# Filler products ahead of the FFN: 11 float32 products of ones replaced by 60 float32r products of real operands

## What is computed

```
    mixed = (jax.nn.sigmoid(g_hg) * y_hg + jax.nn.sigmoid(g_da) * y_da) @ w_out[l]
    x = x + rms_norm(mixed, norm_mix_post[l])

    h = rms_norm(x, norm_ffn_pre[l])
    gate, up = jnp.split(h @ w_ffn_up[l], 2, axis=-1)
    ffn = (jax.nn.silu(gate) * up) @ w_ffn_down[l]
    x = x + rms_norm(ffn, norm_ffn_post[l])
```

## Time and profile before

| | us |
|---|---|
| median of 3 timed runs | 2039.4 (2038.42 to 2040.06) |
| span of the profiled execution | 2038.8 |
| TensorE products busy | 2028.0 (99% of the span) |
| VectorE busy | 1043.2 (51%) |
| ScalarE busy | 820.0 (40%) |
| mean granted TensorE clock | 0.999 of full |

### The profile page before, as it was taken

The page is one execution under the profiler, slowest core; times in us unless marked ns, Lnnn a source line. Parts: engine busy times, 40 slices in busy tenths (PEclk is TensorE's granted clock), DMA queues, the critical chain, the costliest instruction groups (busy, mean ns, idle before and its releaser), DMA issues.

```text
span 2038.8 us, 38346 instructions
## 1 busy us (share of the span) xinstructions
PE 2028.0 (99%) x14816; PEld 1915.0 (94%) x14816; DVE 1043.2 (51%) x1331; ACT 820.0 (40%) x1091; POOL 74.5 (4%) x119
## 2 busy tenths in 40 slices
PE   9999999999999999999999999999999999999999
PEld 9999888888888888899999999999999999999998
DVE  7443555646546465665546744434444445445445
ACT  6233443434434354354345433333333333445444
POOL 1001010000100000000000000000000000000000
PEclk9999999999999999999999999999999999999999
DMA  8867888988889888876544444444444444444441
GB/s 296 167 231 236 306 330 317 355 302 338 331 315 352 306 334 330 319 275 237 171 143 140 151 145 152 132 158 154 153 145 143 145 161 148 145 154 143 155 146 52
DMA packets 123982, 444.13 MB, mean 218 GB/s; under 512 B 14581, under 2 KB 18709, under 8 KB 123856
## 3 DMA queue, kind: packets, MB, share of 16 engines
q1 hardware_dynamic: 112720, 402.31, 55.4%
q0 software_dynamic: 9968, 39.48, 6.6%
q10 hardware_dynamic: 1232, 1.47, 0.2%
HBM read 423.28 MB, written 22.54 MB: 219 GB/s over the span
## 4 chain that ended last, share of the span: by engine, by line
PE 98%; DVE 1%; DMA 1%; ACT 0%; SPq 0%; issue 0%; DVEq 0%
PE ps L407 24%; PE ps L408 24%; PE ps L409 24%; PE ps L1769 5%; PE ps L1770 5%; PE ps L1768 5%; PE ps L881 3%; PE ps L915 3%; PE ps L890 1%; DMA raw<-w_hg 0%; PE ps L707 0%; PE ps L694 0%; DVE ffn L1730 0%; PE ps L667 0%; PE ps L644 0%; PE ps L673 0%
## 5 line engine op out<-in xcount | busy, mean ns | idle before, releaser
L366 DVE TENSOR_TENSOR w_lo<-raw,w_hi 128x1024 fp32r<-128x1024 f32 x416 | 505.4, 1224 | 543.9 <-ACT w_hi L361 289.4
L407 PE MATMUL ps<-x_hi,w_hi 128*128 128x320 f32 x1536 | 485.2, 316 | 1.6 <-DVE w_lo L366 1.6
L408 PE MATMUL ps<-x_hi,w_lo 128*128 128x320 f32 x1536 | 475.3, 309 | 0.0
L409 PE MATMUL ps<-x_lo,w_hi 128*128 128x320 f32 x1408 | 435.0, 309 | 0.0
L407 PE MATMUL ps<-h_hi,w_hi 128*128 128x320 f32 x1400 | 433.1, 309 | 0.0
L408 PE MATMUL ps<-h_hi,w_lo 128*128 128x320 f32 x1400 | 433.0, 309 | 0.0
L409 PE MATMUL ps<-h_lo,w_hi 128*128 128x320 f32 x1400 | 433.0, 309 | 0.0
L361 ACT ACTIVATE w_hi<-raw 128x1024 fp32r<-128x1024 f32 x236 | 247.2, 1059 | 424.5 <-PE ps L409 415.8
L407 PEld LDWEIGHTS ps<-x_hi,w_hi 128*128 128x128 f32 x1536 | 289.1, 188 | 38.6 <-issue 31.6
L408 PEld LDWEIGHTS ps<-x_hi,w_lo 128*128 128x128 f32 x1536 | 289.4, 188 | 0.1
L409 PEld LDWEIGHTS ps<-x_lo,w_hi 128*128 128x128 f32 x1408 | 264.5, 188 | 0.0
(11 more groups left out here) (315 smaller groups left out, 2190.9 us busy)
## 6 DMA issues: line engine op xcount, KB each, us to landing
raw<-w_in SPq DMA_DIRECT2D x176, 512.0 KB, 6.4
raw<-w_up SPq DMA_DIRECT2D x176, 512.0 KB, 3.5
raw<-ck SPq DMA_DIRECT2D x128, 512.0 KB, 6.2
raw<-cv SPq DMA_DIRECT2D x128, 512.0 KB, 6.7
raw<-w_dn SPq DMA_DIRECT2D x88, 512.0 KB, 3.5
raw<-w_out SPq DMA_DIRECT2D x32, 512.0 KB, 3.8
uT<-stage POOLq DMA_DIRECT2D x14, 640.0 KB, 3.9
raw<-w_hg SPq DMA_DIRECT2D x16, 512.0 KB, 4.9
```

The lines of the kernel that those rows point to most:

```text
L366: dve.tensor_tensor(w_lo[half][:, :], raw[slot][:, :], w_hi[half][:, :].bitcast(F32), ALU.subtract).then_inc(lo_ready, 1)
L407: pe.matmul(out, wh[:, c, m, :], xh(c), start=first, stop=False)
L408: pe.matmul(out, wl[:, c, m, :], xh(c), start=False, stop=False)
L409: mm = pe.matmul(out, wh[:, c, m, :], xl(c), start=False, stop=last)
```

## The change

`keep_going(pe, 11)` between `spread_roots` and `pe_first_hidden` becomes `fill_rounded(pe)`. The new function issues ten groups of six products. All have 128 columns of `w_hi[0]` as stationary operand and columns of `m_hi` as moving operand, start PSUM anew each time, and are read by nobody. The groups differ in the width (512, 256, 160, and 320 for the other seven), in the bank (one group alternates between 5 and 7, the rest write to 7), and in where an operand starts: two groups begin at column 8 or 4 of the moving operand, two at column 4 or 8 of the stationary one, one at column 32 of the bank. A wait on `lo_ready` stands ahead of them, the same that opens `pe_first_hidden`. The three earlier products of ones, and the 14 at the kernel's start, stay.

```diff
+        def fill_rounded(pe):
+
+            pe.wait_ge(lo_ready, R_UP + 1)
+            flat = m_hi[:, :, :].rearrange("p k t -> p (k t)")
+            w = w_hi[0][:, :]
+
+            def fill(n, x0=0, w0=0, o0=0, banks=(7,)):
+                for i in range(6):
+                    pe.matmul(ps[:, banks[i % len(banks)], o0:o0 + n], w[:, w0:w0 + P], flat[:, x0:x0 + n],
+                              start=True, stop=True)
+
+            fill(512)
+            fill(256)
+            fill(160)
+            fill(T)
+            fill(T, banks=(5, 7))
+            fill(T, x0=8)
+            fill(T, x0=4)
+            fill(T, w0=4)
+            fill(T, w0=8)
+            fill(T, o0=32)
...
             keep_going(pe, 3)
             pe.wait_ge(e_vec.sem, e_vec.at(0, "rs"))
             e_pe.done(spread_roots(pe, 6), "rs")
-            keep_going(pe, 11)
+            fill_rounded(pe)
             pe_first_hidden(pe)
```

## The result

The changed kernel takes 2045.49 us (median of 5 runs, 2044.67 to 2046.02) against 2039.4 us before (5 runs, 2038.42 to 2040.5): 6.1 us or 0.3% slower, ratio 1.0029 with a 95% interval of 1.0019 to 1.0040. The forecast was 2045.2 in a range of 2043.9 to 2047.5. The profiled execution has a span of 2043.9 us.

What follows compares the result with a forecast made beforehand. TensorE's queue was taken as the bound. A filler of 8.98 us against 3.11 us of room gave +5.87, less 0.07 at the FFN's first product: 2039.4 + 5.8 = 2045.2 us, range 2043.9 to 2047.5.

Steps and rivals of the forecast that it cites:

- The bound: Whole kernel: TensorE's queue sets the time; the FFN's 930.34 us stretch has no gap and can't take up a delay.
- The cover: FFN entry: 3.11 us from the filler's start to the FFN's first product; a filler up to about 3.0 us is free.
- What is removed costs nothing: FFN entry: removing the eleven products of ones (2.72 us) alone gives nothing, as the FFN still starts near 1092.16, behind VectorE.
- The added wait on `lo_ready`: Ahead of the filler: the wait was satisfied over 7 us before, so it costs nothing.
- The sum: The new filler: 1.36 + 0.72 + 0.66 + 6.16 + 0.08 = 8.98 us, so the FFN's first product starts 5.87 us later.
- The first joint: Filler's start: a float32r product right behind float32 ones has a late successor, 0.08 us more for the first filler product.
- rival B: Filler's narrow groups: float32 price at 160 columns, +1.1 us (2046.3); if 256 columns too, 2.1 more (2048.4); chance 0.15.
- The rule for the gap, and the 131 ns: Filler products: the skill's N / 2.4 + 2.5 ns gives 8.1 us; its 131 ns makes the six wide products 0.79 us.
- From the span to the median: Whole kernel: the median lies 0.6 us above the profiled span, which goes from 2038.8 to 2044.6 us.
- C: Filler's displaced products: twice the pitch for 12 gives +1.8 us (2047.0), for all 30 +4.4 us (2049.6); chance 0.11.
- E: Whole filler: repeated operands let products run at streaming time, 7.92 us, 4.8 us more than before (2044.2); chance 0.06.
- D: FFN's 6336 products: the longer lead of VectorE and ScalarE gives 1.7 us back, so within 0.2% of before; chance 0.05.

Runs made afterwards that it cites:

- the narrow row: Changed kernel with its filler made twenty plain products each of 256, 224, 192, 160, 128, 96, 64 and 32 columns: 2059.85 us in one execution.
- the wide row: Changed kernel with its filler made twenty plain products each of 512, 448, 384 and 320 columns: 2050.92 us in one execution.
- the 300: Changed kernel with its filler made 300 products of 320 columns: plain 2079.74 us (ratio 1.0201); in another kernel, all displaced, 2079.52 us (1.0200).

## Why the prediction was right, point by point

**The bound.** TensorE's queue sets the time, and nothing behind the entry takes up a delay. Right: the FFN's stretch is 929.8 us in the kernels before and after, and between 929.76 and 929.85 with 10, 20, 80, 120 or 300 filler products in front of it, as long as the clock stays up.

**The cover.** 3.11 us, right to 0.01 us in two experiments.

**What is removed costs nothing.** Right for the changed kernel, which fills the place in its stead. The sentence said more than that: that taking the ones out alone gives nothing, because a wait is their cover. That step was wrong as a mechanism. Without any filler the clock fell behind 3.04 us of idleness, and the FFN's first 13 distances were up to 0.267 us. What covers TensorE's time does not cover its clock.

**The added wait on `lo_ready`.** Free, as argued from the earlier trace rows: the filler starts 1.00 us after the first record of the roots (1087.23 to 1088.23), as the ones did (1088.05 to 1089.05).

**The sum.** Forecast 8.98 us of filler, measured 9.06. The 42 products of 320 columns: 6.16 forecast, 6.20 measured, with 0.04 more at the first one behind the narrow group. 160 columns: 0.66 and 0.64, since the first distance of the group is shorter by those same 0.04 us, and the load as the limit was the right choice between 0.08 and 0.29 us; the narrow row bears it out down to 96 columns. 256: 0.72 and 0.72. 512: 1.36 and 1.39 without the joint, since the fixed 0.013 us on top grows to 0.020 at this width. The first joint, 0.08 forecast, was 0.11. Three terms came out larger and one smaller, 0.08 us more in all.

**The joint and the ones.** Two readings behind the sum were off, and it hardly felt them. The late successor was put down to a float32r product behind float32 ones. But the removed ones, float32 behind float32, have it too: their second record starts at 1089.27 us, 0.21 behind the first, and the other distances are 0.112. So a product of ones cost 0.223 us and not 0.233, and the float32 price for 160 columns in rival B is 0.28 us and not 0.29. The weight loads of the changed kernel, at the filler's first product and at the FFN's, suggest what the joint is:

```profile
1088.23 0.19 PEld L465 LDWEIGHTS ps<-m_hi,w_hi 128*128 128x128 f32 x1
...
1097.15 0.19 PEld L1472 LDWEIGHTS ps<-h_hi,w_hi 128*128 128x128 f32 x1
```

The filler's first load starts together with its product, and the next load 0.107 us later; the FFN's load starts 0.14 us ahead of its product. A first load that nothing hides adds 0.107 us: 0.107 + 0.147 = 0.254 for 320 columns and 0.107 + 0.233 = 0.340 for 512, which are the first distances of the kernels with 20 products and with the wide row. This is argued from starts; no run was made for it.

**The rule for the gap, and the 131 ns.** The Trainium skill's figures ("TensorE: Matmul & The Clock Gate", section "Back-to-back issue gap") would have made the filler 8.1 us by N / 2.4 + 2.5 ns, and 8.4 by 131 ns for 512 columns; both are estimates worked out from that page. The measurement decides against both for float32r products that load weights each time: 9.06 us, and 0.233 us at 512 columns.

**From the span to the median.** This step was wrong and did no harm. In every execution of which both are known, the time is 1.6 us above the span (2045.49 and 2043.9). The time of the profiled execution of before is not known. If the 1.6 us hold for it too, it was 2040.4 us, and the 0.6 us between its span and the median are 1.6 less 1.0 us by which it ran longer than the median one. Its fall of the clock between 866 and 880 us may be a part of that; it isn't shown to be all. Since the sum was a difference added to the median, the forecast of the time held, while the span was put at 2044.6 and came out at 2043.9. Of the measured 6.1 us, 5.88 are seen at the entry, and 0.2 are within the scatter, so the forecast is right by its terms and not by luck.

**The rivals.** B (narrow at the float32 rate) and C (displaced is slower) are refuted by distances, C to below 0.1 ns for shifts by 4 columns and 32 of the result. E (streaming time alone) is refuted by the 300. D (the FFN gets quicker) is refuted by the doubled filler. None of the four knew of the clock, which turned out to be what a filler's form can decide.

## What to carry to other kernels

A filler in an engine's queue has a cover, which can be read from the timeline: from where it begins to where the next real product can start. Inside it a filler cost nothing in the medians here, beyond it every product costs its distance in a row, here 0.147 us for 320 float32r columns, and nothing gives that back where the engine has no waits behind it. A filler is there for the clock, and its form decides whether it serves: half a cover of 320-column products kept the clock up here, and a row of 64-column products without a gap lost it. If an early product is moved up by reordering its producer, look first at the slack of what that producer makes right after it.

## What the runs showed of the hardware

- A row of products that reads as 100% busy can lose the clock. 120 of 64 columns each at 0.111 us distance: from 1.00 to 0.50 after 5 us in the profiled execution, and a mean clock of 0.992 to 0.994 in all four; 120 of 224 columns each at the same distance: 1.00 over the stretch shown, and a mean of 0.999 or 1.0 in all four.
- A float32r product with a 128-column weight load of its own did not come quicker than 0.111 us in the mean of a group, at 224, 192, 160, 128, 96 and 64 columns alike. At the lower clock the distance is 0.213 us at 64 and 32 columns, so what sets it, the load by the argument above, slows with the granted clock.
- Starts of the moving and the stationary operand at columns 4 and 8, of the result at 32, and alternating banks leave the distance at 0.147 us. With shifts that are no whole 16 bytes it was 0.143 to 0.149, in one execution.
- Over streaming time at 2.4 GHz, a product costs 0.012 to 0.014 us more at 256, 320 and 384 columns, 0.017 at 448 and 0.020 at 512.
- The idle time of 3.04 us ahead of the FFN cost 1.5 us in the profiled execution although it lay wholly under a wait. How much the other nine lost isn't shown; their times lie between 2039.4 and 2042.7 us.
